# Mixer A's raw queries transposed by VectorE and block moves instead of TensorE, with the last gate's blocks split between two engines

## The reference

```
h = rms_norm(x, pre_norm_w)
qa, za, ga, kc, vc, ksl, vsl, kw, vw, qb, kb, vb, zb = split(h @ w_in)
q_raw = q.reshape(b, N_KV_A, GROUP_A, s_len, dh) * scale
q_rot = rope(q, pos) * scale
sc    = einsum('bhgtd,bhcd->bhgtc', q_raw, kc)      # compressed branch, raw queries
p_cmp = softmax(where(c_valid, sc, NEG)) ; o_cmp = p_cmp @ vc
# selected and window branches use q_rot against rotated keys
o   = gates[0] * o_cmp + gates[1] * o_slc + gates[2] * o_win
mix = concat([oa * silu(za), ob * silu(zb)])
out = x + rms_norm(mix @ w_out)
```

## Time and profile before

| | |
|---|---|
| runs, median (range) | 1768.36 us (1768.18 to 1768.87) |
| the profiled execution's own time | 1768.78 us |
| its span, first to last instruction | 1766.8 us, 22876 instructions |
| TensorE matmul busy | 1759.6 us, 7902 matmuls |
| VectorE, ScalarE, GpSimd busy | 1152.4, 883.4, 602.2 us |
| granted TensorE clock, mean | 0.999 |

### The profile page before, as it was taken

The page is one execution under the profiler, slowest core; times in us unless marked ns, Lnnn a source line. Parts: engine busy times, 40 slices in busy tenths (PEclk is TensorE's granted clock), DMA queues, the critical chain, the costliest instruction groups (busy, mean ns, idle before and its releaser), DMA issues.

```text
span 1766.8 us, 22876 instructions
## 1 busy us (share of the span) xinstructions
PE 1759.6 (100%) x7902; PEld 1456.5 (82%) x7902; DVE 1152.4 (65%) x1192; ACT 883.4 (50%) x1208; POOL 602.2 (34%) x842
## 2 busy tenths in 40 slices
PE   9999999999999999999999999999999999999998
PEld 8888888888888888888888888888888888888886
DVE  7657656787888878656665666566655774444445
ACT  7643455463554546456435644564456544444443
POOL 2335303367593948721353034304431520000000
PEclk9999999999999999999999999999999999999999
DMA  8866687656565656666666666666666656666665
GB/s 292 250 203 188 188 247 229 179 166 180 158 187 150 184 158 177 181 195 185 178 195 196 182 180 198 192 190 178 191 192 190 191 180 217 213 213 213 213 202 204
DMA packets 184267, 344.77 MB, mean 195 GB/s; under 512 B 15216, under 2 KB 19568, under 8 KB 184176
## 3 DMA queue, kind: packets, MB, share of 16 engines
q1 hardware_dynamic: 183456, 342.58, 66.0%
q10 hardware_dynamic: 720, 0.93, 0.1%
HBM read 339.27 MB, written 4.19 MB: 194 GB/s over the span
## 4 chain that ended last, share of the span: by engine, by line
PE 88%; DVE 5%; ACT 3%; issue 3%; POOL 1%; ACTq 0%; DVEq 0%
PE acc L637 28%; PE acc L643 28%; PE acc L640 28%; DVE w_parts L1229 2%; ACT w_parts L926 1%; PE acc L818 1%; POOL rot L512 1%; ACT probs L946 0%; PE scores L807 0%; DVE rot_tmp L1503 0%; DVE mixed L1591 0%; PE heads L754 0%; PE scores L774 0%; PE heads L756 0%; PE heads L755 0%
## 5 line engine op out<-in xcount | busy, mean ns | idle before, releaser
L1229 DVE TENSOR_TENSOR w_parts<-raw,w_parts 128x1024 fp32r<-128x1024 f32 x620 | 783.8, 1266 | 558.6 <-ACT w_parts L926 557.1
L926 ACT ACTIVATE w_parts<-raw 128x1024 fp32r<-128x1024 f32 x620 | 656.0, 1059 | 668.2 <-PE acc L643 653.7
L637 PE MATMUL acc<-w_parts,x_parts 128*128 128x512 f32 x2424 | 947.2, 391 | 1.0 <-DVE w_parts L1229 1.0
L643 PE MATMUL acc<-w_parts,x_parts 128*128 128x512 f32 x2424 | 943.7, 389 | 0.0
L640 PE MATMUL acc<-w_parts,x_parts 128*128 128x512 f32 x2424 | 943.3, 389 | 0.0
L643 PEld LDWEIGHTS acc<-w_parts,x_parts 128*128 128x128 f32 x2424 | 455.0, 188 | 95.6
L637 PEld LDWEIGHTS acc<-w_parts,x_parts 128*128 128x128 f32 x2424 | 455.3, 188 | 94.5 <-issue 1.4
L640 PEld LDWEIGHTS acc<-w_parts,x_parts 128*128 128x128 f32 x2424 | 455.3, 188 | 93.1
L512 POOL COPY rot<-tok_b 32x256 f32<-32x256 f32 x128 | 91.1, 712 | 140.9 <-DVE tok_b L1601 135.7
L496 POOL TENSOR_TENSOR rot<-tok_a,trig 128x512 f32<-128x512 f32 x18 | 30.6, 1699 | 260.0 <-ACT tok_a L932 121.4
L512 POOL COPY b_first_t<-probs 32x128 f32<-32x128 f32 x64 | 31.1, 486 | 163.0 <-DVE probs L1672 160.5
(11 more groups left out here) (239 smaller groups left out, 1007.3 us busy)
## 6 DMA issues: line engine op xcount, KB each, us to landing
raw<-in_w_in SPq DMA_DIRECT2D x478, 512.0 KB, 3.6
raw<-in_w_out SPq DMA_DIRECT2D x128, 512.0 KB, 4.4
raw<-in_w SPq DMA_DIRECT2D x16, 512.0 KB, 4.7
x_tok<-in_x SPq DMA_DIRECT2D x16, 256.0 KB, 5.0
xt_raw<-in_x_t SPq DMA_DIRECT2D x7, 512.0 KB, 6.0
wpost<-in_post_w SPq DMA_DIRECT2D x8, 256.0 KB, 5.0
out<-y SPq DMA_DIRECT2D x3, 512.0 KB, 2.8
out<-y SPq DMA_DIRECT2D x5, 256.0 KB, 2.1
```

Of the source, the lines that this page charges most:

```text
L637: nc.tensor.matmul(o, stat_hi, mov_hi, start=(k == 0), stop=False)
L643: last = nc.tensor.matmul(o, stat_lo, mov_hi, start=False, stop=(k == KB - 1))
L926: nc.scalar.activation(w_hi[:, n % SPLIT_SLOTS, :, 0:width], raw[:, n % RAW_SLOTS, :, 0:width], ACT.Copy).then_inc(hi_ready, 1)
L1229: V.tensor_tensor(w_lo[:, s, :, 0:width], raw[:, n % RAW_SLOTS, :, 0:width], w_hi[:, s, :, 0:width].bitcast(F32), ALU.subtract).then_inc(l ...
```

## The change

- TensorE's eight `transpose4` (two in each of four groups) and ScalarE's eight copies from `trans` are gone.
- VectorE transposes `tok_a` in place, in 32 by 32 blocks, at step 0 of the attention frame, ahead of the split of pair 3. GpSimd then moves blocks 0 to 7 to `qraw_t` at the head of `rotate_a`, and ScalarE blocks 8 to 15 at step 1, ahead of its split of pair 4.
- The compressed scores, the cosine products and the crossed halves wait for both movers. The crossed halves of tile 0 stand after the split of step 2 instead of before it.
- In the mixing frames of mixer A, `rest_turned` of unit 1 stands in step 1, between the addition and the first reciprocal of `mix_tile`, instead of ahead of the split of step 2.
- Last gate: GpSimd moves 8 blocks, ScalarE 4 at step 7 and 4 at step 8, each ahead of its split; VectorE's multiplication stands at step 9 instead of 11.

```diff
+                pool.wait_ge(q_turned, g + 1)
+                move_blocks(tok_a[:, :, :].rearrange("p t (h d) -> p t h d", h=HPG),
+                            qraw_t[:, :, :].rearrange("p h (t q) -> p t h q", t=TILES),
+                            range(QUARTERS * QUARTERS // 2)).then_inc(q_moved_pool, 1)
+                pool.wait_ge(q_moved_pool, g + 1)
+                pool.wait_ge(q_moved_act, g + 1)
...
-                if n in (1, 2):
-                    t = n - 1
-                    pe.wait_ge(acc0_free if t == 0 else acc1_free, c)
-                    transpose4(tok_a[:, t, :], fill + t)
                 if n == 3:
-                    pe.wait_ge(tr_free, fill + 2)
+                    pe.wait_ge(q_moved_pool, g + 1)
+                    pe.wait_ge(q_moved_act, g + 1)
...
-                    if at in (1, 2):
-                        take_fill(fill + at - 1, qraw_t[:, :, (at - 1) * P:at * P])
+                    if at == 1:
+                        act.wait_ge(q_turned, g + 1)
+                        for i in range(QUARTERS * QUARTERS // 2, QUARTERS * QUARTERS):
+                            last = move_quarters(tok_a, qraw_t, i // QUARTERS, i % QUARTERS)
+                        last.then_inc(q_moved_act, 1)
...
+                if n - LEAD in (7, 8):
+                    act.wait_ge(mix_turned, 2 * GROUPS)
+                    for cols in range(QUARTERS):
+                        last = move_quarters(tok_b, rot[:, :, :].rearrange("p i (h q) -> p (i h) q", q=SEQ),
+                                             n - LEAD - 5, cols)
+                    if n - LEAD == 8:
+                        last.then_inc(last_moved, 1)
...
-                    if at in (2, 3):
-                        crossed_halves(at - 2, g, fill)
+                    if at == 0:
+                        dve.wait_ge(acc0_free, c)
+                        dve.wait_ge(acc1_free, c)
+                        V.transpose(tok_a[:, :, :], tok_a[:, :, :]).then_inc(q_turned, 1)
                     if at == 3:
+                        crossed_halves(1, g)
...
                     split(c, n)
+                    if at == 2:
+                        crossed_halves(0, g)
...
                     V.tensor_scalar(m, m, 1.0, None, ALU.add).then_inc(silu_step, 1)
+                    if of_a and t == 0:
+                        rest_turned(1, group)
                     dve.wait_ge(silu_step, base + 1)
...
-                if n - LEAD == 11:
-                    turn_mixed(11, 2 * GROUPS - 1, False, 11)
+                if n - LEAD == LAST_MIX_STEP:
+                    turn_mixed(LAST_MIX_STEP, 2 * GROUPS - 1, False, LAST_MIX_STEP)
```

More of the change, by code:

```diff
@@ L87 @@
 LATE_TURN_STEPS = {1: 0, 2: 1, 10: 2, 11: 3, 12: 4, 13: 5}
+LATE_REST_STEPS = {n: u for n, u in LATE_TURN_STEPS.items() if u != 1}
 LATE_VALUE_STEPS = {2: 0, 3: 1, 11: 2, 12: 3, 13: 4, 14: 5}
@@ L507, in _, with move_blocks @@
             pool.wait_ge(trig_ready, 1)
-            def move_blocks(src, dst):
-                for i in range(QUARTERS * QUARTERS):
+            def move_blocks(src, dst, blocks=range(QUARTERS * QUARTERS)):
+                for i in blocks:
                     rows, cols = [slice(v * QUARTER, (v + 1) * QUARTER) for v in divmod(i, QUARTERS)]
@@ L551, in rotate_a, with move_mixed @@
                 pool.wait_ge(q_ready, 2 + 2 * g)
-            def move_mixed(group):
+            def move_mixed(group, blocks=range(QUARTERS * QUARTERS)):
                 pool.wait_ge(mix_turned, group + 1)
@@ L556, in move_mixed @@
                 last = move_blocks(tok_b[:, :, :].rearrange("p t (h d) -> p t h d", h=HPG),
[L557 removed]
+                                   dst.rearrange("p h (t q) -> p t h q", t=TILES), blocks)
                 last.then_inc(mix_moved, 1)
@@ L608, in _ @@
             move_probs_b(GROUPS - 1)
-            move_mixed(2 * GROUPS - 1)
+            move_mixed(2 * GROUPS - 1, range(QUARTERS * QUARTERS // 2))
         @block.tensor
@@ L648, in gemm_pair @@
                     last.then_inc(last_tile0, 1)
[L650 to L655, removed]
             def first_scores(unit, g):
@@ L724, in attention_a, with scores_a @@
                 if n in UNIT_STEPS:
-                    scores_a(UNIT_STEPS[n], g, unit, fill)
-            def scores_a(u, g, unit, fill):
+                    scores_a(UNIT_STEPS[n], g, unit)
+            def scores_a(u, g, unit):
                 t = UNIT_TILES_A[u]
@@ L1494, in rest_turned, with crossed_halves @@
                                 ).then_inc(pt_ready, 1)
-            def crossed_halves(t, g, fill):
-                dve.wait_ge(tr_free, fill + t + 1)
-                if t == 1:
+            def crossed_halves(t, g):
+                if t == 0:
+                    dve.wait_ge(q_moved_pool, g + 1)
+                    dve.wait_ge(q_moved_act, g + 1)
+                else:
                     dve.wait_ge(q_rot_ready, 1 + 2 * g)
@@ L1576, in attention_a_frame, with mix_tile @@
                         turn_pair(3, unit)
-            def mix_tile(at, group):
+            def mix_tile(at, group, of_a=False):
                 if at not in (1, 2, 3, 4, 5, 6):
@@ L1603, in turn_mixed @@
                     dve.wait_ge(mix_moved, group + 1)
+                    if last == LAST_MIX_STEP:
+                        dve.wait_ge(last_moved, 1)
                     dve.wait_ge(heads_done, group + 1)
@@ L1619, in mixing_frame @@
                         turn_pair(5, UNITS_A * group)
-                    if of_a and n - LEAD in LATE_TURN_STEPS:
-                        rest_turned(LATE_TURN_STEPS[n - LEAD], group)
+                    if of_a and n - LEAD in LATE_REST_STEPS:
+                        rest_turned(LATE_REST_STEPS[n - LEAD], group)
                     split(c, n)
-                    mix_tile(n - LEAD, group)
+                    mix_tile(n - LEAD, group, of_a)
                     turn_mixed(n - LEAD, group, of_a)
```

51 lines of the change are left out of this document (24 added, 27 removed).

## The result

| | before | after |
|---|---|---|
| runs side by side, median (range) | 1768.44 us (1768.18 to 1768.87) | 1781.40 us (1781.24 to 1783.10) |
| ratio, with its 95% interval | | 1.0074 [1.0062, 1.0087] |
| the profiled execution's own time | 1768.78 us | 1783.10 us |
| its span | 1766.8 us | 1781.3 us |

Slower by 13.0 us, where 10.6 over the median was forecast (1779.0).

A forecast was written before the change was run, and what follows sets the result against it. TensorE, busy 1759.6 of 1766.8 us, was taken as the bound by a hair (0.32 us slack at pair 7). Frames +11.75, rests -1.2 and last gate -0.3 gave +10.2 on 1768.8: 1779.0 us, range 1770 to 1784.

The forecast's parts named there:

- the forecast's signs of being wrong: Attention frames: compressed scores waiting at pair 3, mask_unit ahead of TensorE at pair 7, or a clock below full.
- The chain: Attention frame: query rotation on VectorE and GpSimd starts at 445.8, ends 3.35 us later than before, delaying mask_unit to 464.07.
- the exclusion behind the 8.8: VectorE and GpSimd exclude each other, so products, sum, splits and crossed halves run one after another, taking 8.8 us.
- The frame terms: Attention frames up to pair 7's scores: 2.45 us longer in group 0, 3.1 in each other group, +11.75 in sum.
- a rival of 0.06: TensorE's clock falls in the new stalls, one pair per frame costing 2.72 us more: 1789.9 us; chance 0.06.
- Last gate: Stall of 1.15 us before pair 14 goes, one at pair 10 comes: -0.3 us, bounds -1.15 and +0.8.
- the forecast's stall of 0.8: Last gate, pair 10: TensorE waits 0.8 us because ScalarE's split stands behind its moves.
- Rests: Mixing frames: unit 1's rest done over 1 us sooner, so TensorE's wait goes: -1.2 us, gain 0 to 1.2.
- Halves first: Attention frames: crossed halves get in ahead of GpSimd's second cosine product, each frame some 1.1 us shorter: 1774.6 us; chance 0.20.
- Engines that don't exclude each other: Attention frames: VectorE and GpSimd overlap in the new order, +0.85 us a frame: 1770.1 us, no change; chance 0.05.
- Full gain: Pair 7: the chain has room and TensorE keeps its gain of 3.84 us: 1762.6 us, faster; chance 0.06.
- a gain of 0.96 a frame: Attention frame: a group's eight transposes leaving TensorE save at most 0.96 us, 3.84 over four groups.

The follow-up runs named there:

- Experiment 1: Kernel before with only unit 1's rest ahead of the reciprocal and the last gate's blocks divided; queries still go by TensorE: 1767.09 us.
- experiment 2: Kernel before with only the first crossed halves moved behind the split of step 2: 1775.96 us.
- 6: Changed kernel with the compressed softmax's second half and its rows' transpose moved to step 8: 1792.79 us.
- 7: Changed kernel with the rotation's products and sums on VectorE, and the compressed softmax's second half and transpose at step 8: 1785.20 us.
- 8: Changed kernel with an own buffer for tile 1's crossed halves, and the compressed softmax's second half and transpose at step 8: 1787.44 us.
- experiment 12: Changed kernel with the rotation on VectorE and the masks of units 0 and 1 ahead of the compressed softmax's second half and transpose: 1775.95 us.
- experiment 5: Changed kernel with the rotation's cosine products and sums on VectorE instead of GpSimd: 1781.38 us.
- experiment 11: Changed kernel, rotation on VectorE, unit 1's scores a pair later, ScalarE moving eight of the sixteen blocks of units 0 and 1: 1803.43 us.
- Experiment 9: Kernel before with the change's rests and last gate, ScalarE's last-gate moves placed behind its splits of pairs 10 and 11: 1766.04 us.
- Experiment 3: Changed kernel with the first crossed halves ahead of the split of step 2 again: 1782.62 us.
- experiment 4: Changed kernel with an own buffer for tile 1's crossed halves, so they don't wait for tile 0's sum: 1779.91 us.
- experiment 10: Changed kernel with the rotation's products and sums on VectorE and unit 1's scores a pair later: 1782.49 us.

## Why the prediction was right

**Where the time goes.** Right: a gap just behind mask_unit at pair 7 in all four frames, no wait at pair 3, the last gate's gap at pair 10 instead of 14. One of the forecast's signs of being wrong came true as well: the clock was below full in two of the frames. Experiment 1 takes the queries out and is faster; experiments 2, 6, 7, 8 and 12 close or open the gap at pair 7 by VectorE's queue alone.

**The chain.** Predicted to start at 445.8 in the frame as of before, that is 7.4 after its first matmul; measured 449.93 - 442.43 = 7.5. It takes 8.78 for 8.8 forecast, and from its end to that of mask_unit 9.46 for 9.48. For the exclusion behind the 8.8, the trace of after has a finer pair of rows. GpSimd's copies, beside VectorE's split and beside its reciprocal (506.91 and 508.03, L1236 and L1602):

```profile
506.91 1.35 POOL L516 COPY qraw_t<-probs_more 32x128 f32<-32x128 f32 x1
...
508.29 1.27 POOL L516 COPY qraw_t<-probs_more 32x128 f32<-32x128 f32 x4
```

One copy takes 1.35 beside the split, which reads two tiles; four take 1.27 together beside the reciprocal, which reads one. Beside a transpose of VectorE's, which reads one too, they take no longer either: 0.29 each from 499.54 to 500.49, with the transpose from 499.51 to 500.76. The Trainium skill, "SBUF — State Buffer", § SBUF: two separate sides, says that a VectorE instruction takes the lock against a reading GpSimd instruction when it has two inputs in SBUF. The trace agrees. So the transposes do not hold up GpSimd's moves, and the splits behind them do: the first move of the raw queries takes 1.23 beside a split, the other seven 0.39 to 0.40.

**The frame terms.** 2.67, 3.29, 3.29 and 3.17 against 2.45 and 3 x 3.1: short by 0.7 in all. In group 1, 0.1 of it is the later start, and 0.1 the time from mask_unit's end to TensorE's start, 0.15 for 0.05.

**The term that was missing.** The forecast priced TensorE's clock as a rival of 0.06 and left it out of the sum. It cost 3.2 us in the profiled execution, most of the 4.1 by which that one, 1783.10, lies over the forecast. The median lies 2.4 over it; its executions have a higher clock on record, and how much of the 2.4 is the clock's is not traced. So it is partly luck that the number came out as near as it did: in how many frames the clock falls stood nowhere in the sum, and two more falls, as in experiment 5, would have added some 3 us. The price was sized wrong too: a whole pair at half the clock, 2.72 us in each frame; it was 7 matmuls in one frame and fewer in the next, 1.7 and 1.4 us, and nothing in two. The traces show no fall behind the four gaps of 1.84 to 1.97 in experiment 2, falls behind 25 of the 45 gaps of 2.26 to 3.29 in the changed kernel and the experiments on it, and behind all four of 3.8 to 4.2 in experiment 11. On this the Trainium skill, "TensorE: Matmul & The Clock Gate", § Part 1, says that the clock goes to 1.2 GHz when the engine has been idle; these runs agree, and add that equal gaps can end either way.

**The small terms.** Rests: -1.4 for -1.2. Last gate: -0.3 for -0.3, with the forecast's stall of 0.8 (1.04 - 0.23) in its place. Experiment 9 shows what the forecast's wording already had: the stall was ScalarE's split queued behind the moves.

**The rivals.** Halves first: it didn't happen. GpSimd's second product starts at 456.18, tile 1's halves at 456.26, and they take 2.45 instead of 1.39, which is the 1.1 a frame of this rival. (Experiment 3 moves tile 0's halves, and there too the second product starts first, by 0.07.) Engines that don't exclude each other: experiment 4's longer rows speak against it. Full gain: nothing came near it. Not tried: a chain that starts as early as before, with the transposes gone.

**The range.** Its upper end, 1784, holds the bound of the rests (+1.2) and not that of the last gate (+1.1); with both it would be 1784.9.

**What stays open.** Which gap makes the clock fall and which doesn't; and what the clock's falls cost in the executions without a trace.

## What to carry to other kernels

Before work is taken off the bounding engine, look for how late its feeders may be at each place where it waits for them: here 0.32 us at pair 7 and, by the estimate of experiment 12, some 0.4 at the values, so that a gain of 0.96 a frame was out of reach for anything that makes VectorE 3.3 us late. Moving the waiter, reordering the feeder's queue or giving a piece to a third engine only showed the next place, since VectorE and ScalarE feed each other's splits and hand a lateness on. And a stall of over 2 us on TensorE should be priced with up to 1.7 us more for the clock behind it, in the sum and not as a remote rival. It can be too high a price: where another engine would stop TensorE a little later anyway, as perhaps in experiment 10, the total hardly changes.

## What the runs showed of the hardware

- TensorE gaps of 1.84 to 1.97 us before pair 7 left the clock full (4 of 4, experiment 2). Of 45 gaps of 2.26 to 3.29, 25 were followed by a fall: 3 to 8 matmuls 0.43 us apart instead of 0.23, 1.4 to 1.8 us in sum. All four gaps of 3.8 to 4.2 (experiment 11) were; behind one of 3.76 it was 12 matmuls. Shortening the stall of pair 6 while that of pair 7 stayed (experiment 5) went with more falls, not fewer.
- GpSimd's 32 by 128 copy takes 0.29 us beside VectorE's reciprocal or its transpose, and 1.35 beside its subtraction of two tiles.
- VectorE alone does the rotation and two splits in 8.24 us, where it and GpSimd together take 8.78 without the last sum and 10.21 with it.
